# Every norm's inverse root: product with 1/D, then logarithm and exponential on ScalarE

## The reference, cut to what matters

```python
def rms_norm(x, g):
    y = xf * lax.rsqrt(jnp.mean(xf * xf, axis=-1, keepdims=True) + EPS)
    return (y * g.astype(jnp.float32)).astype(x.dtype)
# block 1, per layer:  x = x + mixer(rms_norm(x, ..));  x = x + relu(rms_norm(x, ..) @ w_up)**2 @ w_down
#   MLA also norms two low-rank rows: c_q (384 wide) and c_kv (256 wide)
# between the blocks:  x = rms_norm(x, final_norm_g)
# block 2:  h = rms_norm(x, tm_pre_g) * (1 + sc_t) + sh_t;  y = token_mixer(h)
#           x = x + g_t * rms_norm(y, tm_post_g)
#           h = rms_norm(x, cm_pre_g) * (1 + sc_c) + sh_c;  y = conv_ffn(h)
#           x = x + g_c * rms_norm(y, cm_post_g)
# inside the mixer: a layer norm of the convolution (256 wide), and a norm per head
#   (64 wide) of the mLSTM and of the gated linear attention
```

## Time and profile before

| | us |
|---|---|
| median of three runs | 2134.11 |
| the profiled execution | 2135.68 |
| its span | 2134.0 |
| PE busy | 2029.1 (95% of the span) |
| DVE busy | 1160.8 (54%) |
| ACT busy | 815.9 (38%) |
| POOL busy | 29.8 (1%) |
| TensorE's mean granted clock | 0.976 of full |

### The profile page before, as it was taken

One profiled execution on the slowest core, in us unless ns is written; L12 is line 12 of the kernel. 1 busy time (PEld: TensorE's weight loads), 2 busy tenths in 40 slices (PEclk: granted clock), 3 DMA queues, 4 the chain that ended last, 5 costly groups with the idle time before them and its releaser, 6 DMA issues.

```text
span 2134.0 us, 27146 instructions
## 1 busy us (share of the span) xinstructions
PE 2029.1 (95%) x9128; PEld 1612.7 (76%) x9128; DVE 1160.8 (54%) x1606; ACT 815.9 (38%) x1218; POOL 29.8 (1%) x51
## 2 busy tenths in 40 slices
PE   7999999999999999999999899988999969999996
PEld 5777678888876767788888678656888848888885
DVE  5455456565666544543443679475444466654545
ACT  4444443233243343332232443473233246542321
POOL 0000000000000000000000000000000010000001
PEclk9999999999999999999999899989999989999998
DMA  4223135555521111232223223101222212322222
GB/s 136 90 79 88 60 108 177 197 197 187 193 89 57 45 57 59 89 103 94 99 93 104 68 89 98 50 30 65 93 98 98 92 36 88 99 98 99 98 91 76
DMA packets 59179, 206.49 MB, mean 97 GB/s; under 512 B 6797, under 2 KB 7325, under 8 KB 59121
## 3 DMA queue, kind: packets, MB, share of 16 engines
q1 hardware_dynamic: 56736, 198.08, 27.4%
q0 software_dynamic: 1808, 5.56, 1.2%
q10 hardware_dynamic: 576, 2.10, 0.3%
HBM read 203.58 MB, written 2.13 MB: 96 GB/s over the span
## 4 chain that ended last, share of the span: by engine, by line
PE 89%; DVE 5%; ACT 4%; issue 1%; DMA 1%; POOL 0%; DVEq 0%; ACTq 0%; SPq 0%; POOLq 0%
PE bank L644 26%; PE bank L646 26%; PE bank L645 26%; PE bank L755 1%; PE bank L812 1%; PE bank L827 1%; PE bank L738 1%; DVE w_lo L1974 1%; PE bank L781 1%; PE bank L740 1%; ACT w_hi L1298 1%; DVE arena L2043 1%; ACT arena L1628 1%; DVE x L2744 0%; PE bank L1065 0%
## 5 line engine op out<-in xcount | busy, mean ns | idle before, releaser
L644 PE MATMUL bank<-b_hi,w_hi 128*128 128x512 f32 x2560 | 1013.7, 396 | 39.8 <-DVE w_lo L1974 15.0
L645 PE MATMUL bank<-b_lo,w_hi 128*128 128x512 f32 x2560 | 1002.9, 392 | 0.0
L646 PE MATMUL bank<-b_hi,w_lo 128*128 128x512 f32 x2560 | 1002.8, 392 | 0.0
L644 PEld LDWEIGHTS bank<-b_hi,w_hi 128*128 128x128 f32 x2560 | 484.7, 189 | 156.5 <-issue 22.6
L1974 DVE TENSOR_TENSOR w_lo<-w_raw,w_hi 128x1024 fp32r<-128x1024 f32 (+1 forms) x334 | 398.6, 1194 | 354.8 <-ACT w_hi L1298 353.8
L646 PEld LDWEIGHTS bank<-b_hi,w_lo 128*128 128x128 f32 x2560 | 484.4, 189 | 102.0
L645 PEld LDWEIGHTS bank<-b_lo,w_hi 128*128 128x128 f32 x2560 | 485.3, 190 | 100.6 <-issue 2.0
L1298 ACT ACTIVATE w_hi<-w_raw 128x1024 fp32r<-128x1024 f32 (+1 forms) x334 | 343.1, 1028 | 336.7 <-PE bank L646 310.4
L2056 DVE TENSOR_TENSOR x<-bank,x 128x512 f32 (+1 forms) x80 | 55.1, 691 | 135.7 <-PE bank L646 135.7
L1507 ACT ACTIVATE arena<-arena 128x512 f32<-128x512 f32 x64 | 40.5, 632 | 201.2 <-DVE arena L2220 201.2
L2765 DVE SCALAR_TENSOR_TENSOR arena<-bank,vec,arena 128x511 f32<-128x511 f32 x88 | 65.9, 749 | 88.5 <-ACT arena L1914 82.7
(11 more groups left out here) (282 smaller groups left out, 1322.2 us busy)
## 6 DMA issues: line engine op xcount, KB each, us to landing
w_raw<-in_wstream SPq DMA_DIRECT2D x308, 512.0 KB, 3.2
arena<-in_ada SPq DMA_DIRECT2D x48, 512.0 KB, 3.4
w_raw<-in_wstream SPq DMA_DIRECT2D x16, 384.0 KB, 3.0
arena<-crow POOLq DMA_DIRECT2D x16, 256.0 KB, 4.9
w_raw<-in_wstream SPq DMA_DIRECT2D x10, 256.0 KB, 2.7
x<-in_xT ACTq DMA_DIRECT2D x4, 512.0 KB, 7.5
out_xT<-x SPq DMA_DIRECT2D x8, 256.0 KB, 2.0
arena<-in_cvec POOLq DMA_DIRECT2D x1, 512.0 KB, 4.0
```

Source lines behind the costliest of these rows:

```text
L644: nc.tensor.matmul(dst, whi, rhs_hi(k), start=(k == 0), stop=False)
L645: nc.tensor.matmul(dst, whi, rhs_lo(k), start=False, stop=False)
L646: last = nc.tensor.matmul(dst, wlo, rhs_hi(k), start=False, stop=(k == n - 1))
```

## The change

The matrix of ones becomes a matrix of 1/D (`mean_sq`), so that one product leaves the mean on every partition. Where the width is not D, the squares are scaled as ACT makes them. `halves`, the matrix for the heads, gets its 1/64 too. Then `inverse_root` makes the inverse root on ACT by two activations: a logarithm out of the bank, and an exponential with scale -0.5. ACT waits for its own logarithm in between. DVE's reciprocals and the way by token (columns, spreading products, the copy) are gone; DVE only waits (`root_set`). POOL waits for the same semaphore. PE's waits for the reader of `c_bank` are now on `norm_rstd`, and `head_squares` has a new wait for the reader of its bank. `ready_root` is a table load written by hand, of the set with both functions; it stands also ahead of the layer norm's root, of the first head root, after the last projection's Silu and ahead of the small exponential `row_floors`, which moves from tile 6 to tile 8, past the sigmoids. The set with Silu is loaded by hand ahead of the last FFN.

```diff
-            def root(norm, width, bias=eps):
-                if NORM[norm]:
-                    act.wait_ge(norm_rstd, NORM[norm])
+            roots = Steps(root_ln)
+            def inverse_root(dst, mean, bias, done):
+                act.wait_ge(root_ln, roots.mark(act.activation(dst, mean, ACT.Ln, bias=bias)))
+                act.activation(dst, dst, ACT.Exp, scale=-0.5).then_inc(done, 1)
+            def root(norm, dst=rstd, bias=eps):
                 act.wait_ge(norm_sum, NORM[norm] + 1)
-                dst, src = (std_col, c_bank[:, 0:QB]) if norm in BY_TOKEN else (std, c_bank[:])
-                act.activation(dst, src, ACT.Sqrt, bias=bias, scale=1.0 / width).then_inc(norm_std, 1)
+                inverse_root(dst, c_bank[:], bias, norm_rstd)
             def ready_root():
-                act.activation(small[:, 63:64], eps, ACT.Sqrt)
+                act.preload_act_table_set("natural_log_exp_and_others")
...
-            def reciprocal_root(norm, dst=rstd):
-                dve.wait_ge(norm_std, NORM[norm] + 1)
-                dve.reciprocal(dst, std).then_inc(norm_rstd, 1)
+            def root_set(norm):
                 dve.wait_ge(norm_rstd, NORM[norm] + 1)
...
-                if norm in BY_TOKEN:
-                    sum_by_token(squares).then_inc(norm_sum, 1)
-                    rstd_row(norm)
-                else:
-                    nc.tensor.matmul(c_bank[:], ones_sq[:], squares, start=True, stop=True).then_inc(norm_sum, 1)
+                nc.tensor.matmul(c_bank[:], mean_sq[:], squares, start=True, stop=True).then_inc(norm_sum, 1)
...
-            def add_normed(n0, scale, row):
-                dve.tensor_copy(rstd, row).then_inc(rstd_set, 1)
-                dve.wait_ge(rstd_set, n0 // (KT // 2) + 1)
+            def add_normed(n0, scale):
...
             def conf_root():
                 act.wait_ge(ln_var, 1)
-                act.activation(ml_s_std, c_bank[:], ACT.Sqrt, bias=eps, scale=1.0 / MIX).then_inc(ln_std, 1)
+                ready_root()
+                inverse_root(ml_s_std, c_bank[:], eps, ln_std)
...
-                act.activation(dst, src[:], ACT.Sqrt, bias=eps, scale=1.0 / DH).then_inc(head_std, 1)
+                inverse_root(dst, src[:], eps, head_std)
...
-            before = {4: lambda: log_sigmoid((row_b,), one[0:HEADS, :], row_abs, row_ln), 6: row_floors}
+            before = {4: lambda: log_sigmoid((row_b,), one[0:HEADS, :], row_abs, row_ln), 8: row_floors}
...
             def head_norm(i, src, root, dst, gain, gates):
                 dve.wait_ge(head_std, i + 1)
-                own(dve.reciprocal(root, root))
...
             def head_squares(i, src, dst):
+                if i >= 2:
+                    pe.wait_ge(head_std, i)
                 pe.wait_ge(head_sq, i + 1)
...
             modulate(KT, 3, 4)
+            act.preload_act_table_set("silu_and_others")
```

More of the change, by code:

```diff
@@ L628, in _ @@
             for i in range(2):
-                pool.wait_ge(rstd_set, i + 1)
+                pool.wait_ge(norm_rstd, NORM[("mix_y", "ffn_y")[i]] + 1)
                 with pool.Fori(0, KT // 2) as half:
@@ L700, in sum_squares @@
                 else:
-                    pe.wait_ge(norm_std, NORM[norm])
+                    pe.wait_ge(norm_rstd, NORM[norm])
                     pe.wait_ge(ctx_lo, CTX0["mla"] + (MLA_HEADS if NORM[norm] >= NORM["ff_b"] else 0))
-                if norm in BY_TOKEN:
-                    sum_by_token(squares).then_inc(norm_sum, 1)
-                    rstd_row(norm)
-                else:
-                    nc.tensor.matmul(c_bank[:], ones_sq[:], squares, start=True, stop=True).then_inc(norm_sum, 1)
[L710 to L724, removed]
+                nc.tensor.matmul(c_bank[:], mean_sq[:], squares, start=True, stop=True).then_inc(norm_sum, 1)
             def logits(n, m):
@@ L1041, in feature_sum @@
                 for i in range(2):
-                    last = nc.tensor.matmul(c_bank[:], ones_sq[:], src[i], start=(i == 0), stop=(i == 1))
+                    last = nc.tensor.matmul(c_bank[:], mean_sq[:], src[i], start=(i == 0), stop=(i == 1))
                 last.then_inc(done, 1)
@@ L1270, in _ @@
             sum_squares("mix_y", PREP0["mix_y"] + KT)
-            pe.wait_ge(norm_std, NORM["cm"])
+            pe.wait_ge(norm_rstd, NORM["cm"])
             for k in range(KT):
                 pe.wait_ge(cm_sq, k + 1)
-                last = nc.tensor.matmul(c_bank[:], ones_sq[:], sq[k % 2], start=(k == 0), stop=(k == KT - 1))
+                last = nc.tensor.matmul(c_bank[:], mean_sq[:], sq[k % 2], start=(k == 0), stop=(k == KT - 1))
                 last.then_inc(cm_added if k < KT - 1 else norm_sum, 1)
@@ L1340, in prepare @@
                                    scale=g_col)
-                act.activation(sq[s], src, ACT.Square).then_inc(prep_hi, 1)
+                act.activation(sq[s], src, ACT.Square, scale=(D / width) ** 0.5).then_inc(prep_hi, 1)
             def x_tile(k):
@@ L1384, in _ @@
             split(1, 0, PANEL, 1)
-            root("fox", D)
+            root("fox")
             def exponentials(n, m):
@@ L1520, in start @@
             def start(norm):
-                root(norm, D)
+                root(norm)
                 if norm == "ff_a":
@@ L1536, in _ @@
             split(half0 + 1, 0, PANEL, t0 + 1)
-            root("mla", D)
+            root("mla")
             def prepare_low(norm, n, at, tile0):
@@ L1630, in _ @@
             modulate(0, 0, 1)
-            root("final", D)
+            root("final", rstd_f)
             def read(i, dst, func, scale=1.0):
@@ L1664, in conf_squares @@
                     act.wait_ge(ln_dev, i + 1)
[L1665 removed]
+                    act.activation(ml_v[i], conf_u[i], ACT.Square, scale=(D / MIX) ** 0.5).then_inc(ln_sq, 1)
             def conf_root():
                 act.wait_ge(ln_var, 1)
[L1669 removed]
+                ready_root()
+                inverse_root(ml_s_std, c_bank[:], eps, ln_std)
             def conf_high():
@@ L1886, in _ @@
                 split(half0, s, PANEL, t0 - 1 + s)
-            root("mix_y", D)
+            root("mix_y")
             for k in range(KT):
@@ L1959, in _ @@
             lead0()
-            root("ffn_y", D)
+            root("ffn_y")
         @block.vector
@@ L2242, in ffn @@
                         now = add_to_x(t0), last_post if c == FF_CHUNKS - 1 else nothing
-                    segment(run, i * KT, KT, *now, lead0, lead1, (lambda: reciprocal_root(norm)) if i == 0 else None,
+                    segment(run, i * KT, KT, *now, lead0, lead1, (lambda: root_set(norm)) if i == 0 else None,
                             beside=beside if 1 <= i < 7 else None)
@@ L2269, in _ @@
             split(half0 + 1, 0)
-            reciprocal_root("mla")
+            root_set("mla")
             def prepare_low(norm, n, at):
@@ L2415, in modulate @@
                        .then_inc(h_lo, 1)
-            modulate(0, row)
+            modulate(0, rstd)
             def head_gates():
@@ L2509, in conf_low @@
                        .then_inc(ln_lo, 1)
-            def conf_reciprocal():
-                dve.wait_ge(ln_std, 1)
-                own(dve.reciprocal(ml_s_std, ml_s_std))
             def gates_by_key():
@@ L2827, in _ @@
             lead1()
-            add_normed(KT // 2, 5, reciprocal_by_token("ffn_y"))
+            root_set("ffn_y")
+            add_normed(KT // 2, 5)
 def kernel(**inputs):
```

61 lines of the change are left out of this document (26 added, 35 removed).

## The result

The changed kernel took 2123.68 us (median of five runs, 2119.72 to 2126.05) against 2135.83 for the kernel before in its five runs. The ratio is 0.9941 with a 95% interval of 0.9925 to 0.9957: 12.6 us faster, 9 to 16. The forecast was 13.0 us off 2134.1. The same kernel run a second time gave 2122.89, ratio 0.9938 (0.9926 to 0.9951).

What follows compares the result with a forecast made beforehand. PE was taken as the bound, with 89% of the chain of waits, so a root counts only where PE or the tail waits. Terms summed to 13.0 us off 2134.1, giving 2121.1 us, range 2115.5 to 2127.5.

Steps and rivals of the forecast that it cites:

- x2: Norm where PE waits for the root: product to first use 4.61 to 3.49 us, gain 1.1, 1.06 more at full clock.
- mix_y: Norm whose scaling waits for the root: gain 2.95 us, ACT's panel copies becoming the new bound.
- ffn_y: Last norm, ahead of the tail: product to first use 3.60 to 2.43 us, gain 1.2.
- latent attention: At its start, without DVE's second reciprocal, PE's next tile comes 2.1 us earlier; half the half-clock cost goes, 0.85.
- forget gates: One table load between exponential and logarithm leaves the path; gain 0.8 us.
- ff_a, ff_b: At these two norms PE's next weights wait less for DVE's read; 0.4 us each, 0.8 together.
- mixer: Four reciprocals and four loads leave; net 0.1 us early, and 0.9 from the wait at 1476.87 closing.
- final norm: ACT's root stands ahead of a panel copy PE waits for, and the exponential delays it: a loss of 0.7 us.
- Only the open norms pay: Rival: gains only where nothing else is in flight, later waits taking over the rest; 2126.8 us, chance 0.12.
- ACT's queue as the bound: Rival: sixteen exponentials hold back copies and reads PE needs, making the kernel slower; 2140.1 us, chance 0.03.
- The clock gives more: Rival: less half clock at the first logits, latent attention and chunk work gives 4.2 us more; 2116.9 us, chance 0.09.
- Loads forced back: Rival: other ACT functions force table sets back, some six loads at the four open norms; 2128.9 us, chance 0.03.

Runs made afterwards that it cites:

- after: The changed kernel itself, the whole change made to the kernel before; 2123.68 us, ratio 0.9941.
- run 1: The changed kernel again with no edit, for a second profile; 2122.89 us, ratio to the kernel before 0.9938.
- run 3: The kernel before, three norms summed by one full-tile product instead of by token, square root and reciprocal kept; 2140.60 us, ratio 1.0022.
- run 7: The changed kernel with every root's logarithm made twice; 2127.15 us, ratio to the kernel before 0.9953.
- run 9: The changed kernel with two table loads put ahead of the logarithm at four roots without cover; 2133.38 us, ratio to the kernel before 0.9981.
- run 5: The kernel before with only the three norms around the start of the latent attention on logarithm and exponential; 2132.27 us, ratio 0.9971.
- run 4: The changed kernel with ACT's root of the final norm moved behind the copy of the next panel; 2115.17 us, ratio to the kernel before 0.9906.
- run 2: The kernel before with only five norms (x2, final, mix_y, cm, ffn_y) on one product, logarithm and exponential; 2127.90 us, ratio 0.9960.
- run 6: The changed kernel with two table loads in every turn of the last FFN's three loops; 2120.93 us, ratio to the kernel before 0.9925.
- run 8: The changed kernel with the final root behind the panel copy and the first head root behind the last denominators; 2114.19 us, ratio to the kernel before 0.9896.

## Why the prediction was right, term by term

The forecast's sum against the two profiles (the distance between the same two instructions of PE, before less after) and the runs:

| term | forecast | profiles | shown by |
|---|---|---|---|
| x2 | 1.1 (2.2 at full clock) | 2.05 | run 1: 1.1 at half clock |
| mix_y | 2.95 | 3.00 | runs 3, 7 |
| cm | 2.7 | 2.49 (root to use 2.73) | run 7 |
| ffn_y | 1.2 | 1.06 | runs 7, 9 |
| latent attention, to the next tile + clock behind it | 2.1 + 0.85 | 1.98 + 0.98 | run 5 |
| forget gates | 0.8 | 0.9 | seven traces without the load, four with it |
| ff_a, ff_b | 0.8 | 0.44 + 0.46 | seven traces with the new root, four with the old |
| mixer, `ready_root` | 0.1 + 0.9 + 0.2 | 1.68 | not shown as a sum |
| final norm | -0.7 | -0.62 | run 4 |
| not forecast | | 1.34 at 821 to 861, clock; 0.24 in small pieces | not shown |
| sum | 13.0 | 16.0 | |

**What held.** The price of a root's new path on ACT (1.38 us) was exact, since both parts had rows of their own form. At mix_y the norm no longer holds up the scaling alone: it ends 0.04 us ahead of DVE's work on the panels (forecast 0.06). The loss at the final norm came, and so did the new wait for the denominators.

**Forget gates.** From PE's first product to its wait at the first logits' products it is 43.36 us before and 43.79, 44.33, 43.84 in runs 2, 3 and 5, which keep the load there. In after and in runs 1, 4, 6, 7, 8 and 9 it is 42.47, 42.85, 43.38, 43.01, 43.03, 42.07 and 42.18. The means differ by 1.1, but single pairs need not (43.36 and 43.38): seven traces with the same instructions here spread over 1.3 us.

**ff_a and ff_b.** From PE's wait at 282.73 to the one at 635.73, which is ff_a, it is 353.0 us in before and in runs 2, 3 and 5, and 352.6 to 352.7 in the other seven traces. For ff_b (861.15 to 1210.32) it is 349.2 in these four and 348.7 to 348.8 in the seven. So 0.3 to 0.4 at each is shown, and the wait of PE's weight loads in the earlier trace rows is gone.

**What was less sure than it looks.** In the latent attention the next tile starts 1.98 us earlier (forecast 2.1); it waits 0.41 for its low part, which the forecast had as its bound there. The 0.85 for the clock was half of a price, because the forecast couldn't tell whether the stretch would go. It went wholly; a part of its cost lay ahead of the tile, so 0.98 came out behind it. That the half came so near is luck.

**The mixer.** Its waits did what was told: the 0.70 ahead of the transposes and the 0.75 at 1476.87 are gone, 0.64 at the denominators is new, and the 5.01 for the states stayed. The sum I can't show. From the panel behind the final norm to the product at mix_y it is 487.23 us before and 485.55 after, but 485.20, 489.73 and 490.45 in runs 1, 6 and 9, whose instructions there are the same: the clock moves this part by 5 us, and a term of 1.2 drowns in it. PE's idle time alone, added up over the same part, is 18.14 us before and 17.67 after, 0.5 less; but it is 17.39 in run 3, which has the mixer of before. So the 1.2 stays unshown, and may be half of that. Before has a stretch at 1442 that after lacks, after has one at 1376 that before lacks.

**Why the profiles say 16.0 and the ratio of the medians 12.6.** Two places of after's first profile make 2.3 of it: no half clock at 821 (1.34), and a product at full clock at x2 (0.95). The other runs left no trace, so that they lacked these two isn't shown, and the remaining 1.1 isn't placed. The clock fits. Its other four runs had a mean granted clock of 0.976 to 0.977, the profiled one 0.980; over 2120 us 0.003 in the mean is 13 us more at half clock, which costs PE 6 us at most; the profiled run and the median are 4 apart. In the window from 1370 to 1460 alone the granted clock was 0.87, 0.87, 0.87, 0.83, 0.87, 0.81 and 0.80 in after and runs 1, 4, 6, 7, 8 and 9; in after and runs 1, 4, 6 and 9 PE's waits there are the same within 0.2 us.

**Rivals.** *Only the open norms pay*: out by run 5. *ACT's queue as the bound*: seven roots have no cover (run 7), not sixteen, and for slower the forecast had needed more than twelve. *The clock gives more*: the median (2123.68, and 2122.89 in run 1) isn't the 2116.9 of this rival. But its pieces came in part, which the forecast had outside its sum. At the first logits the stretch is 6.8 us before and after, and 3.4 in runs 1, 4, 6, 7 and 9, where PE needs 183.5 to 183.7 us from there to its wait near 237, against 184.1 to 184.9 with the longer one. In the latent attention the stretch went wholly. In the chunk work there is less half clock in after and in runs 1 and 4, and more in runs 6 and 9. *Loads forced back*: the trace has the 17 loads of the written order and none between logarithm and exponential.

## What to carry to other kernels

A reciprocal of a full tile on DVE cost five times what an exponential on ACT did, so an inverse root by logarithm and exponential pays where the root is waited for. Before choosing the way by which a sum gets to all partitions, price the function at its end: with the reciprocal the short route lost 2.8 us at three places in the traces, with the exponential the same three gained 6.1. Then look at the queue behind the root: an engine that waits there for a product holds back copies that need nothing of it. Moving one line past that wait gave some 7 us by the medians (4.9 in the traces), where the whole rewrite had given 12.6. To find which roots are open, double one cheap step at all of them and read which waits grow.

## What the runs showed of the hardware

- A table load costs its 1.28 us and 0.01 more, also twice in a row and between dependent steps (run 9); 38 of them in a loop where ACT waits 2.52 us for PE cost nothing (run 6).
- PE's waits from x2 on repeat to 0.03 us between two profiles of the same kernel (after and run 1), and the half-clock stretches don't; five to eleven runs of one kernel spread over 3 to 9 us. One stretch came at 1371 to 1377 in after and in runs 1, 4 and 9, and at 1383 in run 2, each some 150 us behind PE's last wait over 0.4 us, and not in runs 6, 7 and 8; its cause stays open.
- Where PE waits ahead of the next step, a stretch is not all loss: the mixer's transposes start 19.33 us behind the start of ACT's copy ahead of them in before and in run 2. PE waited 0.70 us for them in before, with a stretch of 3.4 us at 1404.5, and 2.30 in run 2, without that stretch:

```profile
1419.26 1.09 PE L1036 MATMUL bank<-ident,arena 128*128 128x128 f32 x8 [2.30 <-ACT arena L1645]
```
